# The per-layer embedding's product in the routing chain, a feature-major merge, and VectorE's program written out

## The reference

```python
h = rmsnorm(x, attn_norm)
parts = split(h @ w_in)          # attention, GLA and DeltaNet inputs, and gate_logits (3 x 1024)
y_a, y_b, y_c = window_attention(...), gated_linear_attention(...), gated_delta_rule(...)
gates = sigmoid(gate_logits.reshape(B, S, 3, D))
merged = gates[:, :, 0] * (y_a @ w_br_a) + gates[:, :, 1] * (y_b @ w_br_b) + gates[:, :, 2] * (y_c @ w_br_c)
x = x + merged @ w_o
x = x + hierarchical_moe(rmsnorm(x, ffn_norm), ...)    # group of 4, then 2 of its 8 experts, ff 512
x = x + sigmoid(rmsnorm(x, ple_norm) @ w_ple_gate) * (p[i] @ w_ple)   # p: 256 tokens x 256
```

## Time and profile before

| | us |
|---|---|
| median of 3 runs | 1817.88 (1816.4 to 1820.63) |
| the profiled execution | 1817.57 |
| its span, first to last instruction | 1815.9 |
| PE busy | 1453.6 (80%) |
| DVE, ACT, POOL busy | 395.4, 219.2, 36.2 |
| DMA | 501.34 MB, mean 276 GB/s |
| mean granted TensorE clock | 0.903 of 2.4 GHz |

### The profile page before, as it was taken

One profiled execution on the slowest core, in us unless ns is written; L12 is line 12 of the kernel. 1 busy time (PEld: TensorE's weight loads), 2 busy tenths in 40 slices (PEclk: granted clock), 3 DMA queues, 4 the chain that ended last, 5 costly groups with the idle time before them and its releaser, 6 DMA issues.

```text
span 1815.9 us, 18517 instructions
## 1 busy us (share of the span) xinstructions
PE 1453.6 (80%) x7324; PEld 735.8 (41%) x7325; DVE 395.4 (22%) x756; ACT 219.2 (12%) x419; POOL 36.2 (2%) x34
## 2 busy tenths in 40 slices
PE   7999999997656766676989999999977566665678
PEld 6667645552212221222476676454522122221223
DVE  3442514134000000000234324141430000000002
ACT  1222212110000000000212222111100000000001
POOL 0011000000000000000000110000000000000000
PEclk9999999999878887888989999999988788878889
DMA  7332033298999999999442320433899999999991
GB/s 251 117 139 93 1 139 139 96 376 350 420 421 421 421 421 421 421 421 400 138 153 93 139 93 4 143 132 126 346 394 420 421 421 421 421 421 421 421 403 42
DMA packets 98430, 501.34 MB, mean 276 GB/s; under 512 B 7746, under 2 KB 10308, under 8 KB 48068
## 3 DMA queue, kind: packets, MB, share of 16 engines
q1 hardware_dynamic: 98068, 498.79, 68.4%
q0 software_dynamic: 304, 1.76, 0.2%
HBM read 499.47 MB, written 1.05 MB: 276 GB/s over the span
## 4 chain that ended last, share of the span: by engine, by line
PE 55%; DMA 29%; SPq 10%; DVE 2%; issue 1%; ACT 1%; DVEq 0%; ACTq 0%
PE ps L683 24%; DMA work<-in_w_gate_e 10%; DMA work<-in_w_up_e 10%; SPq L587 10%; DMA work<-in_w_down_e 9%; PE ps L1145 6%; PE ps L704 5%; PE ps L1006 5%; PE ps L1183 2%; PE ps L837 1%; PE ps L1127 1%; PE ps L849 1%; PE ps L1133 1%; PE ps L853 1%; ACT work L1243 1%
## 5 line engine op out<-in xcount | busy, mean ns | idle before, releaser
L683 PE MATMUL ps<-ring,hT 128*128 128x512 f32 (+2 forms) x1088 | 443.5, 564 | 5.5 <-DVE hT L1547 5.5
L1145 PE MATMUL ps<-work 128*32 128x512 f32 x1536 | 261.1, 843 | 190.9 <-DMA work<-in_w_gate_e 95.4
L683 PEld LDWEIGHTS ps<-ring,hT 128*128 128x128 f32 x1088 | 200.6, 191 | 226.3 <-issue 222.3
L1243 ACT ACTIVATE work<-ps 128x512 f32<-128x512 f32 (+3 forms) x208 | 110.1, 554 | 1134.2 <-PE ps L1168 395.5
L1145 PEld LDWEIGHTS ps<-work 128*32 128x32 f32 x1536 | 60.4, 147 | 388.4 <-issue 160.3
L1554 DVE SCALAR_TENSOR_TENSOR work<-work,ps 128x512 f32<-128x512 f32 (+1 forms) x52 | 37.9, 728 | 620.6 <-ACT work L1243 620.6
L1145 PE MATMUL ps<-ring,work 128*32 128x512 f32 x512 | 86.5, 837 | 71.5 <-DMA ring<-in_w_gate_e 46.8
L1183 PE MATMUL ps<-work 128*32 128x512 f32 x768 | 99.1, 662 | 37.6 <-DMA work<-in_w_down_e 30.7
L1006 PE MATMUL ps<-ring,work 128*128 128x512 f32 x192 | 84.7, 594 | 2.9 <-ACT work L1243 2.9
L704 PE MATMUL ps<-hT,ring 128*128 128x256 f32 x384 | 83.7, 380 | 1.8 <-DVE hT L1547 1.8
L1145 PEld LDWEIGHTS ps<-ring,work 128*32 128x32 f32 x512 | 23.1, 147 | 134.9 <-issue 134.9
(11 more groups left out here) (267 smaller groups left out, 980.1 us busy)
## 6 DMA issues: line engine op xcount, KB each, us to landing
work<-in_w_gate_e SPq DMA_DIRECT2D x96, 1024.0 KB, 26.3
work<-in_w_up_e SPq DMA_DIRECT2D x96, 1024.0 KB, 26.7
work<-in_w_down_e SPq DMA_DIRECT2D x96, 1024.0 KB, 26.6
ring<-in_w_in SPq DMA_DIRECT2D x26, 2048.0 KB, 8.0
ring<-in_w_up_e SPq DMA_DIRECT2D x32, 1024.0 KB, 26.6
ring<-in_w_gate_e SPq DMA_DIRECT2D x32, 1024.0 KB, 25.2
ring<-in_w_down_e SPq DMA_DIRECT2D x32, 1024.0 KB, 27.1
ring<-in_w_o SPq DMA_DIRECT2D x4, 2048.0 KB, 8.1
```

The source lines that it names most:

```text
L683: last = mm(ps[:, bank, at:at + n], hT[:, k, t * P:(t + 1) * P], w[:, k, c0:c0 + n], start=(k == 0), stop=(k == w.shape[1] - 1))
L1145: last = mm(ps[CAP * j:CAP * (j + 1), bank, :], xgT[:, 4 * c + k, CAP * j:CAP * (j + 1)], in_slot(n)[:, j, k, :], start=(c + k == 0), stop ...
L1243: return nc.scalar.activation(*args, **kw)
```

## The change

- **p x w_ple.** w_ple is no longer a static chunk. It has a place of its own behind the router's weights and is loaded right after them, ahead of the expert prefetch. PE transposes p between w_o's third and fourth product; ACT copies it in the middle of its sums of squares. PE makes the four p x w_ple products during routing: three after the router, one after the position sums. ACT copies each to `pw`, which lies in `tab` over the tables that only the part before the experts uses.
- **Tables.** They are therefore sorted: first the ones that ACT and the first steps need, then those of the experts, then the attention's, which POOL fetches anew in each layer (1.05 MB), after the last use of `pw`.
- **Zeroing.** ACT zeroes the four banks of sums by copying a zero tile (2 instructions), PE no longer does.
- **Merge.** Gate and branch products are feature-major: the weights are stationary, hT or yT moves, 256 columns (all tokens) at a time; a bank holds two feature blocks. The merged tile is then transposed already; its transposes, ACT's copies and their semaphores go. The factor 0.5 moves to the add of w_o's product to x. w_o is loaded with k outermost to fit. The products of token tile 0 are ordered by k, each group as soon as its merges are done. The expert prefetch waits for the last merge.
- **End of the layer.** The four gate products go to four banks of their own; the w_ple products are gone from there. DVE takes tile 0's transposes before it adds tile 1.
- **Loops.** The layer loops of DVE and POOL are written out for both layers; those of SP, PE and ACT stay.

```diff
-    ("w_ple_gate", 0, 512), ("w_ple_gate", 512, 512), ("w_ple", 0, 1024),
+    ("w_ple_gate", 0, 512), ("w_ple_gate", 512, 512),
...
+EXPERT_TABLES = ("ones", "before", "place", "iota32", "desc32", "desc4")
...
-    merged = scratch.take(T, D, at=9 * 1024)
+    mergedT = bt.rearrange("p t n -> p (t n)").rearrange("p (k n) -> p k n", k=KT)
...
+    w_ple = ring_flat[:, 2 * SLOT + KT * 36:2 * SLOT + KT * 36 + 2 * D].rearrange("p (k n) -> p k n", k=2)
...
-    pinT = act_h.rearrange("p (k n) -> p k n", k=2)
+    pinT = sb("pinT", [P, 2, SEQ])
+    pw = tab[:, KEPT_N:KEPT_N + T * D].rearrange("p (t n) -> p t n", t=T)
...
SP:
+                if name == "w_o":
+                    src = src.rearrange("l (k p) n -> p (l k) n", p=P)
...
+            sp.dma_start(w_ple, one(a["w_ple"], L).rearrange("l (p k) n -> (l p) k n", k=2)).then_inc(s_wple.sem, 16)
...
-            sp.wait_ge(s_mT.sem, s_mT.at(L, 4))
+            sp.wait_ge(s_mg.sem, s_mg.at(L, 12))
...
-            sp.wait_ge(s_routed.sem, L + 1)
-            load_static(J_PLE)
POOL:
-        with pool.Fori(0, L_N) as L:
+        for L in range(L_N):
+
+            pool.wait_ge(s_pg.sem, s_pg.at(L, 4))
+            pool.dma_start(tab[:, KEPT_N:], a["tables"][:, KEPT_N:]).then_inc(s_att.sem, 16)
+            pool.wait_ge(s_att.sem, 16 * (L + 1))
PE:
+            def gate_product(j, i):
+
+                w = slot_view(j)
+                for b in range(2):
+                    c0 = (2 * i + b) * P
+                    for k in range(KT):
+                        last = mm(ps[:, i, b * SEQ:(b + 1) * SEQ], w[:, k, c0:c0 + P], hT[:, k, :],
+                                  start=(k == 0), stop=(k == KT - 1))
+                return last
...
+            for ready, ks in ((10, range(4)), (11, range(4, 6)), (12, range(6, KT))):
+                pe.wait_ge(s_mg.sem, s_mg.at(L, ready))
                 for f in range(2):
+                    last = wo_product(0, f, 4 + f, ks)
+                    if ready == 12:
+                        last.then_inc(s_wo.sem, 1)
+            wo_product(1, 0, 1, range(KT)).then_inc(s_static_used.sem, 1)
+
+            pe.wait_ge(s_pin.sem, 16 * (L + 1))
+            for k in range(2):
+                for t in range(T):
+                    last = tr(ps[:, 0, (2 * k + t) * P:(2 * k + t + 1) * P], pin[:, t, k:PLE:2], ident)
+            last.then_inc(s_pl_p.sem, 1)
+
+            pe.wait_ge(s_x.sem, s_x.at(L, 1))
+            transpose_tile(1, x_block, 0)
+            wo_product(1, 1, 3, range(KT)).then_inc(s_static_used.sem, 1)
...
+            ple_product(0, 6)
+            ple_product(1, 7)
+
+            pe.wait_ge(s_rt.sem, s_rt.at(L, 1))
+            ple_product(2, 4)
 
             pe.wait_ge(s_ch.sem, L + 1)
...
+            pe.wait_ge(s_pw.sem, s_pw.at(L, 2))
+            ple_product(3, 7)
...
                 for f in range(2):
-                    i = 2 * t + f
-                    b = 2 * (i % 2)
                     need(J_PG0 + f)
...
+                    token_major(J_PG0 + f, t, 2 * t + f, 0, 512).then_inc((s_pg_p, s_static_used)[t].sem, 1)
+                    if t + f == 0:
 
                         pe.wait_ge(s_x.sem, s_x.at(L, 2 * T))
...
                         transpose_tile(2, x_block, 1)
ACT:
+            take_ple(0, 6)
+            take_ple(1, 7)
+            take_ple(2, 4)
+            act.wait_ge(s_rt.sem, s_rt.at(L, 2))
+            fn(e2, e2, ACT.Exp).then_inc(s_rte.sem, 1)
+            take_ple(3, 7)
+            act.wait_ge(s_x.sem, s_x.at(L, 2))
+            act.wait_ge(s_init.sem, L + 1)
+            for t in range(T):
+                last = fn(ps[:, 2 * t:2 * t + 2, :].rearrange("p a (b n) -> p (a b) n", n=SEQ),
+                          selwT.unsqueeze(1).broadcast_to([P, 4, SEQ]), ACT.Copy)
+            last.then_inc(s_sums0.sem, 1)
DVE:
-        with dve.Fori(0, L_N) as L:
+        for L in range(L_N):
...
+                    xs = x[:, t, f * 512:(f + 1) * 512]
+                    last = stt(out=xs, in0=ps[:, (4 + f, 1 + 2 * f)[t], :], scalar=0.5, in1=xs, op0=ALU.mult, op1=ALU.add)
...
-            for t in range(T):
                 take_hT(2, "ple_norm", t)
...
-                twice_gated(e, e, ps[:, 2 * (i % 2) + 1, :])
+                twice_gated(e, e, pw[:, t, f * 512:(f + 1) * 512])
```

More of the change, by code:

```diff
@@ L123, in _tables @@
     at, off, parts = {}, 0, []
-    for name, a in sorted(t.items(), key=lambda item: item[0] not in FIRST_TABLES):
+    for name, a in sorted(t.items(), key=lambda item: (item[0] not in FIRST_TABLES, item[0] not in EXPERT_TABLES)):
         at[name] = (off, a.shape[1])
@@ L132 @@
 FIRST_N = sum(TABLE_AT[name][1] for name in FIRST_TABLES)
+KEPT_N = FIRST_N + sum(TABLE_AT[name][1] for name in EXPERT_TABLES)
 INV_FREQ = np.float32(1.0) / np.float32(500000.0) ** (np.arange(0, ROT, 2, dtype=np.float32) / np.float32(ROT))
@@ L241, in _build @@
     tmpA = A.take(T, 512)
+    bt = A.take(T, 1024)
     tmpk = scratch.take(T, 512)
@@ L276, in _build @@
     beta_parts = tmpA[:, 0, 0:SEQ]
-    merged = scratch.take(T, D, at=9 * 1024)
+    mergedT = bt.rearrange("p t n -> p (t n)").rearrange("p (k n) -> p k n", k=KT)
     kswap = scratch.take(T, P, at=11 * 1024)
+    lr_parts = scratch.take(SEQ, at=11 * 1024 + 768)
+    ba_b = A.take(256, at=A.size - 256)[0:1, :]
     kTa = scratch.take(SEQ, at=11 * 1024 + 256)
@@ L309, in _build @@
     hgT = M.take(FT, P)
+    selwT = M.take(SEQ)
+    pin = M.take(T, PLE)
     lg = M.take(T, 36)
@@ L538, in slot_loaded @@
     def slot_loaded(L, j):
-        return 16 * (L * (NS // 3) + j // 3 + 1)
+        return 16 * (L * len(range(j % 3, NS, 3)) + j // 3 + 1)
     @block.sync
@@ L1012, in merge_first @@
                 pe.wait_ge(s_yT.sem, s_yT.at(L, n + 1))
-                for t in range(T):
-                    branch_product(t, 0, jg).then_inc(s_gt_p.sem, 1)
+                for i in range(2):
+                    branch_product(i, 0, jg).then_inc(s_gt_p.sem, 1)
             def merge_second(n, jg):
@@ L1198, in _ @@
                     expert_round(pp, 2 * pp, r)
-            pe.wait_ge(s_pin.sem, 16 * (L + 1))
-            for k in range(2):
-                for t in range(T):
-                    last = tr(ps[:, 6, (2 * k + t) * P:(2 * k + t + 1) * P], pin[:, t, k:PLE:2], ident)
-            last.then_inc(s_pl_p.sem, 1)
             pe.wait_ge(s_ye.sem, 2 * last_pair + 3)
@@ L1431, in _, with take_ple @@
             table_of(ACT.Sqrt)
[L1432 to L1445 removed]
+            rms_of_x(1)
+            def take_ple(i, bank):
+                t, f = divmod(i, 2)
+                act.wait_ge(s_pw_p.sem, s_pw_p.at(L, i + 1))
+                fn(pw[:, t, f * 512:(f + 1) * 512], ps[:, bank, :], ACT.Copy).then_inc(s_pw.sem, 1)
+            act.wait_ge(s_rt.sem, s_rt.at(L, 1))
+            fn(lg[:, :, 0:GROUPS], lg[:, :, 0:GROUPS], ACT.Exp).then_inc(s_rte.sem, 1)
+            take_ple(0, 6)
[10 more added lines that the diff above has]
+            last.then_inc(s_sums0.sem, 1)
             act.wait_ge(s_tbl.sem, L + 1)
```

164 lines of the change are left out of this document (70 added, 94 removed).

## The result

The changed kernel takes 1793.44 us (median of 4 runs, 1792.47 to 1800.35) and the kernel before 1817.14 (4 runs on the same chip, 1815.98 to 1820.63): the ratio is 0.987 (95% interval 0.9853 to 0.9888), the gain 23.7 us. On another chip the same two kernels gave 0.989 (0.9867 to 0.9913; medians of 1801.08 and 1818.28), or 17.2 us. The forecast was 1789.0, with a range of 1781 to 1800.

What follows compares the result with a forecast made beforehand. PE time was taken to bound the kernel outside the expert stretches, bytes inside them, plus the gaps between. Terms -2.4 - 1.6 - 5.0 - 15.6 - 4.0 = -28.6 took the profiled 1817.57 us to 1789.0, range 1781 to 1800.

Steps and rivals of the forecast that it cites:

- the likeliest case: Whole kernel: the forecast itself holds, 1789.0 us, own range 1785 to 1793; chance 0.65.
- Expert stretch: Expert weight stream: w_ple's 1.05 MB moves ahead of the prefetch into a DMA pause, -2.5 us per layer.
- End of layer: Layer's end: gate product starts 0.9 us sooner, four p x w_ple products leave (-6.9); -7.8 us per layer.
- Turn: Layer 1 to layer 2: writing out VectorE's loop removes its 5.82 us gap; first product 4.0 us earlier, once.
- the rival of PE's own turn: Layer turn: PE's loop stalls up to 9 us unseen, or VectorE's gap stays, so no gain: 1793 us; chance 0.12.
- the rival of 109 us per layer: Gates and branches: doubled weight loads are not hidden, +109 us per layer, 2007 us; chance 0.01.
- p: Before w_o's last product: p lands at 378.1, PE asks at 378.8; fits by 0.7 us, cost taken as 0.
- the 3.3 us go with nothing in their place: Between last gate product and w_o: the wait for tanh, merge and transposes vanishes, 3.3 us per layer.
- Part 1: Merge and w_o: wait and p transposes net -2.9 us, 256-column products +0.6, p's landing 0, per layer.
- Part 2: Routing: fourth p x w_ple product +0.7 us, zeroing 0, clock -0.8 in layer 1 and 0 in layer 2.
- they fit by 0.5: Routing: three p x w_ple products, 5.2 us, fit within VectorE's 5.7 us chain before the position sums.
- router, products and gather all at the lower one: Routing rival: all three at 1.2 GHz in both layers, some +5 us per layer, 1799 us; chance 0.08.

Runs made afterwards that it cites:

- x_late_need: Changed kernel with PE's wait for w_o's second half moved to the first product that reads it: 1792.02 us, ratio 0.9845 to the kernel before.
- late p: Changed kernel with POOL asking for p after the second of w_o's products instead of the first: 1796.26 us, ratio 0.9878 to the kernel before.
- last step: Five unread products behind each layer's last gate product, added to the kernel with three wait/routing edits and two unread scan products: 1783.09 us, ratio 0.9806.
- x_narrow: Changed kernel with routing's four p x w_ple products cut to one 32-column matmul each, result left out: 1801.31 us, ratio 0.9906 to the kernel before.

## Why the prediction was right, and where it was not

The time and the likeliest case came out; two steps of Parts 1 and 2 failed.

**Right.** *Expert stretch*: w_ple out of the saturated stream, forecast 2.5 per layer, measured 2.5 and 2.3, at an unchanged 421 GB/s. *End of layer*: forecast 7.8, measured 7.64; the gate products take 28.6 us (forecast 28.4). *Turn*: forecast 4.0, measured 4.1, and 3.4 and 3.9 by undoing and doing it alone. That kills the rival of PE's own turn: PE starts 5.2 us after its last product, 0.06 behind VectorE. *Feature-major products*: forecast +0.6 per layer; from the first merge product to the last gate product's end the two traces have 143.45 and 144.14, +0.69. The weight loads are hidden, and with them the rival of 109 us per layer is gone. *p*: PE asks at 377.49, and p, asked for at 369.20 and 7.0 us on its way, had landed at 376.2: a fit by 1.3 us, forecast 0.7 (from 11.8 us to the first product's end, where 14 of 16 k are 12.0 by the earlier trace rows).

**Failed: "the 3.3 us go with nothing in their place"** (Part 1). Something took their place: 1.14 and 0.98 us of waiting for w_o's second half. I had checked that the merges were ready, not when the weights came. The half is issued at 348.77, when the branch product (L1034) ahead of the last gate product has used up its slot; that is one product of 6.91 us ahead of PE's need, and the half takes 7.7 us. The row for the landing of such a slot, 8.0 us, stood in the earlier trace rows, and I used it at the turn but not here. This step brought 1.6 and 1.8 of the forecast 2.9 (1.0 and 1.1 of the table plus 0.7 for the 256-column products); moving one wait gives 1.3 back per layer.

**Failed: routing** (Part 2). Forecast: -0.1 in layer 1 and +0.7 in layer 2; measured +2.0 and +2.3. The step that failed is "they fit by 0.5": three products of 1.73 behind a router of 1.99. I had named the mechanism and put it in the wrong case: I let router and products run at the full level in layer 1, and gave a chance of 0.08 to router, products and gather all at the lower one. In both layers the lower clock lasted 6.8 us and took in the router's second half and most of the first product. In layer 1 the router took 3.42 us, 1.4 more than before, and the three products 7.12 for 5.2, so that the third ended 1.2 us after the chosen experts were ready (399.85, 398.67). The fourth then held the gather from 401.85, when VectorE had the selection, to 402.68: 0.8, for 0.7 forecast. The zeroing on ScalarE, taken as covered, was not quite: 0.74 and 0.52 us ahead of the first expert product, since PE reads its counts only after that wait. Against this the gather ran at its full speed in both layers, 3.58 us, which the earlier trace rows had at 5.46. The loss is not fixed by the program alone: with the same routing code the trace of `x_late_need` took 1.6 us less per layer, with the router at 1.98.

**Sum.** The failed steps cost 1.3 + 2.1 in layer 1 and 1.1 + 1.6 in layer 2: 6.1 us of forecast gain that did not come. The profiled execution hid about half of it, since its layer 1 ran the scan 3.2 us faster than the kernel before did, at the full clock behind the pause; that is luck and no part of the forecast. The second trace of the same kernel ran that stretch in 201.06, 5.4 us more, and layer 2's 2.1 us more. These 7.5 of the 9.5 us between the two traces are the likely reason why 23.7 us on one chip were 17.2 on another. By its stretches the change is worth about 22 us, which lies between the two.

**Open.** Why the clock falls after the 2 us pause in some executions and not in others is not settled. Nor is the late p's effect on the median, nor why the routing of the changed kernel has 6.8 us of the lower clock in one version and none in another, nor the 1.4 us of the last step that no stretch shows.

## What to carry to other kernels

When a reordering removes a wait, list every input of the instruction that moves forward, the weights in flight too, with issue time and landing time; ask for each at the product that reads it. Price work put on TensorE in a stretch full of waits with the clock in mind: what fills a pause can cost nothing (the two products in the scan), the same kind of product ahead of a step that is due holds it up (the fourth, 0.8 us), and taking it away may gain next to nothing (0.3). Compare stretches cut at the same landmarks before medians: here a gain of 4 us was plain in the trace and lost in a spread of 11.

## What the hardware showed that I had not expected

- Behind a pause of PE of 2 us the lower clock cost 3.2 us (198.8 against 195.65 for the same work) in 20 of 24 scans, and 1.7 us of products that nobody reads, put into the pause, brought 4.9 us in the median. Fourteen such products in all, two in each layer's scan and five at each layer's end, took the kernel from 1792.19 to 1783.09.
- The lower clock lasted 3.4, 6.8 or 13.7 us in the routing: 6.8 in the changed kernel, 3.4 in `x_late_need` with the same routing code, 13.7 in both layers of `x_narrow`, where PE had the least to do.
- Loads of 128x128 f32 weights (190 ns) vanish behind matmuls 216 ns apart over all 768 + 384 records of the gates and branches, up to 0.69 us per layer.
- The turn of VectorE's loop costs 5.3 to 5.8 us, while ScalarE's at the same place shows a gap of 0.2 (906.22 to 906.42 in before). PE's is hidden by its wait.
